# First block of a two-block layer: query and key head norms moved into the first stick-breaking steps, gate halves respaced over both attention loops, stick-breaking branch projected ahead of the latent one

## What is computed

```python
u = rms_norm(h, mix_norm[i])
proj = u @ w_in[i]
c_q, c_kv, k_rope, sb_qkv, gates = jnp.split(proj, SPLITS, axis=-1)
q = (rms_norm(c_q, q_latent_norm[i]) @ w_q_up[i])        # 8 heads of 96
kv = (rms_norm(c_kv, kv_latent_norm[i]) @ w_kv_up[i])    # 8 heads of 64 + 64
q = rms_norm(q, q_head_norm[i]); k = rms_norm(k, k_head_norm[i])
# rotary on the last 32 of each head, then causal softmax attention -> o_mla
sq, sk, sv = ...                                          # 8 heads of 64
o_sb = stick_breaking_attention(sq, sk, sv)
g_mla, g_sb = jnp.split(jax.nn.sigmoid(gates), 2, axis=-1)
merged = g_mla * (o_mla @ w_branch_mla[i]) + g_sb * (o_sb @ w_branch_sb[i])
h = h + merged @ w_out[i]
```

## Time and profile before

| | |
|---|---|
| median of 3 runs | 1412.13 us (1408.71 to 1412.49) |
| profiled execution | 1411.69 us, of which 1409.8 us are the span |
| TensorE busy | 1337.0 us (95%) |
| VectorE busy | 942.5 us (67%) |
| ScalarE busy | 767.1 us (54%) |
| GpSimd busy | 202.6 us (14%) |

### The profile page before, as it was taken

The page is one execution under the profiler, slowest core; times in us unless marked ns, Lnnn a source line. Parts: engine busy times, 40 slices in busy tenths (PEclk is TensorE's granted clock), DMA queues, the critical chain, the costliest instruction groups (busy, mean ns, idle before and its releaser), DMA issues.

```text
span 1409.8 us, 23082 instructions
## 1 busy us (share of the span) xinstructions
PE 1337.0 (95%) x9022; PEld 1217.7 (86%) x9022; DVE 942.5 (67%) x1369; ACT 767.1 (54%) x1150; POOL 202.6 (14%) x165
## 2 busy tenths in 40 slices
PE   9999999999899999999978997989999999999998
PEld 8999989879888999988977887879999877777876
DVE  6555574485476555566379674674675799999996
ACT  5433355664455333456354766324744577777774
POOL 1111120030001221110021321420001000202020
PEclk9999999999999999999989999989999899999999
DMA  9655535522346555544523332315364499999991
GB/s 314 209 179 182 191 122 177 185 90 68 120 150 192 181 182 189 169 135 147 189 89 122 119 124 98 101 38 176 124 210 154 163 409 369 335 367 339 374 332 58
DMA packets 73943, 263.44 MB, mean 187 GB/s; under 512 B 8320, under 2 KB 9600, under 8 KB 73728
## 3 DMA queue, kind: packets, MB, share of 16 engines
q1 hardware_dynamic: 72864, 260.39, 54.3%
q10 hardware_dynamic: 992, 1.86, 0.4%
HBM read 261.17 MB, written 1.05 MB: 186 GB/s over the span
## 4 chain that ended last, share of the span: by engine, by line
PE 59%; DVE 13%; ACT 6%; issue 2%; POOL 1%; DVEq 0%; ACTq 0%; POOLq 0%
PE bank L561 18%; PE bank L563 17%; PE bank L562 17%; DVE sb_wlo L518 3%; DVE sb_wlo L505 3%; DVE sb_XC L2103 1%; PE bank L2754 1%; ACT sb_Uh L636 1%; ACT sb_aw L1713 1%; ACT sb_whi L489 1%; PE bank L2811 1%; PE bank L653 1%; PE bank L741 0%; ACT sb_XC L1684 0%; PE bank L2729 0%
## 5 line engine op out<-in xcount | busy, mean ns | idle before, releaser
L505 DVE TENSOR_TENSOR sb_wlo<-sb_raw,sb_whi 128x1024 fp32r<-128x1024 f32 (+2 forms) x304 | 384.0, 1307 | 206.9 <-ACT sb_whi L489 206.7
L489 ACT ACTIVATE sb_whi<-sb_raw 128x1024 fp32r<-128x1024 f32 (+3 forms) x308 | 301.8, 1031 | 242.4 <-PE bank L563 236.0
L561 PE MATMUL bank<-sb_Uh,sb_whi 128*128 128x256 f32 x1216 | 349.0, 287 | 6.0 <-ACT sb_sgh L1677 2.5
L562 PE MATMUL bank<-sb_Ul,sb_whi 128*128 128x256 f32 x1216 | 344.9, 284 | 0.0
L563 PE MATMUL bank<-sb_Uh,sb_wlo 128*128 128x256 f32 x1216 | 344.9, 284 | 0.0
L561 PEld LDWEIGHTS bank<-sb_Uh,sb_whi 128*128 128x128 f32 x1216 | 234.3, 193 | 10.4 <-issue 6.3
L562 PEld LDWEIGHTS bank<-sb_Ul,sb_whi 128*128 128x128 f32 x1216 | 234.3, 193 | 0.9
L563 PEld LDWEIGHTS bank<-sb_Uh,sb_wlo 128*128 128x128 f32 x1216 | 234.1, 193 | 0.0
L561 PE MATMUL bank<-sb_whi,sb_Uh 128*128 128x256 f32 (+3 forms) x560 | 163.9, 293 | 6.7 <-DVE sb_Ul L645 4.9
L562 PE MATMUL bank<-sb_wlo,sb_Uh 128*128 128x256 f32 (+3 forms) x560 | 161.7, 289 | 0.0
L563 PE MATMUL bank<-sb_whi,sb_Ul 128*128 128x256 f32 (+3 forms) x560 | 161.5, 288 | 0.0
(11 more groups left out here) (405 smaller groups left out, 2261.0 us busy)
## 6 DMA issues: line engine op xcount, KB each, us to landing
sb_raw<-in_slabs SPq DMA_DIRECT2D x162, 512.0 KB, 4.7
sb_raw<-in_ffn_in SPq DMA_DIRECT2D x88, 512.0 KB, 4.5
sb_raw<-in_moe_in SPq DMA_DIRECT2D x50, 512.0 KB, 5.8
sb_raw<-in_ffn_out SPq DMA_DIRECT2D x44, 512.0 KB, 3.9
sb_raw<-in_moe_out SPq DMA_DIRECT2D x26, 512.0 KB, 6.1
sb_deep_free<-in_moe_in SPq DMA_DIRECT2D x16, 512.0 KB, 5.5
sb_deep_uh<-in_moe_in SPq DMA_DIRECT2D x16, 512.0 KB, 5.4
sb_deep_ul<-in_moe_in SPq DMA_DIRECT2D x16, 512.0 KB, 6.1
```

The source lines that it names most:

```text
L489: nc.scalar.activation(whi[:, i % NSLOT, c], raw[:, i % NSLOT, c], ACT.Copy).then_inc(S("hi_done"), 1)
L505: nc.vector.tensor_tensor(wlo[:, i % NSLOT, c], raw[:, i % NSLOT, c], whi[:, i % NSLOT, c].bitcast(F32), ALU.subtract).then_inc(S("lo_done ...
L561: pe.matmul(o, lh, rh, start=start, stop=False, skip_group_check=True)
L562: pe.matmul(o, lh, rl, start=False, stop=False, skip_group_check=True)
```

## The change

It edits orders and tables. (1) ScalarE squares the query heads before the loop: token tile 0 ahead of the split behind the query copies, token tile 1 between the key and value copies of tile 0 and of tile 1. VectorE sums them and GpSimd takes their root ahead of the loop. (2) The key squares and sums move to steps 0 and 1, query scaling, gain and rotation to steps 2, 3 and 4, the key's to 5, 6 and 7. (3) Gate halves: seven instead of six in the stick-breaking loop, at steps 0, 1, 2, 4, 6, 8 and 10, and nine instead of ten in the latent attention, at -1, 0, 1, 3, 4, 6, 7, 8 and 9; copies and splits follow (`gate_seen`, `late_seen`). (4) Gate 3 and the turned heads use other banks. (5) The stick-breaking branch is projected ahead of the latent one in each pair, with slabs to match.

```diff
@@ -124,7 +124,7 @@
     for i in range(2):
-        for nm, w in (("mla", "w_branch_mla"), ("sbr", "w_branch_sb")):
+        for nm, w in (("sbr", "w_branch_sb"), ("mla", "w_branch_mla")):
             add(f"{nm}{i}", w, i * 512, (i + 1) * 512, 4)
@@ -1354,10 +1354,12 @@
-        gate_bank = (6, 7, 6, 7, 2, 7, 2, 7)
-        gate_half_at = {0: (0, 0), 1: (0, 1), 2: (1, 0), 3: (1, 1), 5: (2, 0), 7: (2, 1)}
-        gate_seen = {2: 0, 4: 1, 8: 2}
-        qt_bank, kt_bank = (0, 1, 6, 7), (2, 3, 0, 1)
+        gate_bank = (6, 7, 6, 6, 2, 7, 2, 7)
+        gate_half_at = {0: (0, 0), 1: (0, 1), 2: (1, 0), 4: (1, 1), 6: (2, 0), 8: (2, 1), 10: (3, 0)}
+        gate_seen = {2: 0, 5: 1, 9: 2}
+        late_half_at = {-1: (3, 1), 0: (4, 0), 1: (4, 1), 3: (5, 0), 4: (5, 1), 6: (6, 0), 7: (6, 1), 8: (7, 0), 9: (7, 1)}
+        late_seen = {0: 3, 1: 4, 4: 5, 7: 6, 9: 7}
+        qt_bank, kt_bank = (0, 1, 2, 7), (3, 2, 7, 4)
@@ -1529,6 +1531,8 @@
                                    ACT.Copy).then_inc(S("q_ev"), 1)
+            act.wait_ge(*reach("q_ev", 4))
+            act_head_squares("hq", Q1, MH, QK, None, (0,))
             hi_upto("kvup")
@@ -1536,7 +1540,8 @@
                     act.activation(V1[:, t, 4 * half:4 * half + 4, :], b[:, :, NOPE:P], ACT.Copy).then_inc(S("kv_ev"), 1)
-            act.wait_ge(*reach("q_ev", 4))
+                if t == 0:
+                    act_head_squares("hq", Q1, MH, QK, None, (1,))
             act.wait_ge(*reach("kv_ev", 8))
@@ -1560,10 +1565,8 @@
                 if i < 2:
-                    act_head_squares("hq", Q1, MH, QK, None, (i,))
-                elif i < 4:
                     act.wait_ge(*reach("krope", 1))
-                    act_head_squares("hk", K1[:], MH, QK, ("hq_red", 2), (i - 2,))
+                    act_head_squares("hk", K1[:], MH, QK, ("hq_red", 2), (i,))
                 if i in gate_seen:
@@ -1578,10 +1581,10 @@
             def gates_seen(i):
-                if i % 2 == 0 and 0 <= i < 10:
-                    g = 3 + i // 2
+                if i in late_seen:
+                    g = late_seen[i]
                     gate_out(g)
-                    hi_upto(f"gate{g + 1}" if g < 7 else "mla0")
+                    hi_upto(f"gate{g + 1}" if g < 7 else "sbr0")
@@ -1592,7 +1595,7 @@
             for q in range(4):
-                hi_upto(f"sbr{q // 2}")
+                hi_upto(f"mla{q // 2}")
                 act.wait_ge(*reach("mg_s", q + 1))
@@ -1927,6 +1930,7 @@
             dve.wait_ge(*reach("ld_pb", 16))
+            dve_head_sums("hq", MH, QK)
             lo_upto("gate0")
@@ -1943,20 +1947,20 @@
                                              ALU.add).then_inc(S("sb_m"), 1)
-                if i < 4:
-                    dve_head_sums(("hq", "hk")[i // 2], MH, QK, (i % 2,))
+                if i < 2:
+                    dve_head_sums("hk", MH, QK, (i,))
+                elif i == 2:
+                    dve_head_rsqrt("hq", Q1, MH, QK)
+                elif i == 3:
+                    dve_head_gain("hq", Q1, MH, QK, "q_head_norm")
                 elif i == 4:
-                    dve_head_rsqrt("hq", Q1, MH, QK)
-                elif i == 5:
-                    dve_head_gain("hq", Q1, MH, QK, "q_head_norm")
-                elif i == 6:
                     dve.wait_ge(*reach("rope1", 2))
                     dve_rope("hq", Q1, MH, NOPE, ROPE // 2, COS1, SIN1)
+                elif i == 5:
+                    dve_head_rsqrt("hk", K1[:], MH, QK)
+                elif i == 6:
+                    dve_head_gain("hk", K1[:], MH, QK, "k_head_norm")
                 elif i == 7:
-                    dve_head_rsqrt("hk", K1[:], MH, QK)
-                elif i == 8:
-                    dve_head_gain("hk", K1[:], MH, QK, "k_head_norm")
-                elif i == 9:
                     dve.wait_ge(*reach("hq_turn", 6))
@@ -1972,14 +1976,14 @@
             def gates_low(i):
-                if i % 2 == 1 and 0 < i < 11:
-                    g = 3 + i // 2
-                    lo_upto(f"gate{g + 1}" if g < 7 else "mla0")
+                if i - 1 in late_seen:
+                    g = late_seen[i - 1]
+                    lo_upto(f"gate{g + 1}" if g < 7 else "sbr0")
...
             for q in range(4):
-                lo_upto(f"sbr{q // 2}")
-                used(dve, f"sbr{q // 2}")
+                lo_upto(f"mla{q // 2}")
+                used(dve, f"mla{q // 2}")
                 dve.wait_ge(*reach("gsig", 4))
@@ -2376,11 +2380,12 @@
                 pool_rsqrt(v, v, n, "lat_r")
+            pool_head_rsqrt("hq", MH, QK)
             for i in range(8):
...
                 pool.tensor_tensor(aw[:, 2 + i % 2], aw[:, 2 + i % 2], const("earlier"), ALU.mult).then_inc(S("sb_spm"), 1)
-                if i in (1, 3):
-                    pool_head_rsqrt(("hq", "hk")[i // 2], MH, QK)
+                if i == 1:
+                    pool_head_rsqrt("hk", MH, QK)
             pool_norm("n3")
@@ -2549,12 +2554,12 @@
             def gates_beside(i):
-                if i < 9:
-                    gate_half(3 + (i + 1) // 2, (i + 1) % 2)
+                if i in late_half_at:
+                    gate_half(*late_half_at[i])
...
             for j in range(2):
-                for nm, oh, ol, b0, done in (("mla", OMh, OMl, 0, "mg_a"), ("sbr", OSh, OSl, 4, "mg_b")):
+                for nm, oh, ol, b0, done in (("sbr", OSh, OSl, 4, "mg_b"), ("mla", OMh, OMl, 0, "mg_a")):
                     pe.wait_ge(*reach("mla_olo" if nm == "mla" else "os_lo", 4))
```

## The result

| | before | after |
|---|---|---|
| median | 1411.34 us (4 runs, 1408.71 to 1412.49) | 1401.41 us (4 runs, 1399.77 to 1402.78) |
| profiled execution | 1411.69 us | 1399.77 us |
| ratio of the times | | 0.9929, 95% interval 0.9917 to 0.9942 |

A forecast was written before the change was run, and what follows sets the result against it. TensorE, busy 95%, was taken as the bound, so only waits and slow clock could go: 4.29 + 6.20 - 0.75 = 9.74 us off the profiled 1411.69, plus 0.44 to the median, gives 1402.4 us, range 1399 to 1406.5.

The forecast's parts named there:

- End of the latent attention: Latent tail and first branch projection: waits of 3.74 us and slow clock of 2.46 go, 6.20 us off.
- End of the stick-breaking loop: Head turns and last value pairs: waits of 2.84 us and slow clock of 1.45 go, 4.29 us off.
- The second step: End of the stick-breaking loop: a gate half of 2.97 us is longer than the 1.86 us wait it must cover.
- the banks: Turned query and key heads in other banks: covered by the gate half of step 10, costed at nothing.
- Start of the loop: First gate half: an added query square delays ScalarE's copy freeing bank 6; 0.75 us lost, bounds 0.75 to 1.6.
- The sum: Whole kernel: 4.29 + 6.20 - 0.75 = 9.74 us off, giving 1402.4 us; chance 0.66.
- Middle of the loop: Mid stick-breaking loop: VectorE in time despite earlier work, tightest at step 6's score pair, margin 1.1 or 0.3 us; no cost.
- Rival C: Stick-breaking steps 3 to 7: VectorE late where splits run beside GpSimd; 3 us back, 1405.4 us; chance 0.12.
- End of the branch projections: VectorE's merge sets the 1.78 us wait and both ends move alike; nothing gained, nothing lost.
- B: Head turns: the clock still falls if the transposes alone cause it; 1.45 us stays, 1403.8 us; chance 0.10.
- D: Latent projection: OMl or its slab late, TensorE waits, clock falls again; 6.20 us stay, 1408.6 us; chance 0.09.
- E: Latent steps: ScalarE's and VectorE's steps outlast TensorE's, each head pays; slower, 1418.4 us at 2 us a head; chance 0.03.

The follow-up runs named there:

- e1: The kernel before with only the branch order turned round, stick-breaking ahead of latent; median 1405.63 us, ratio 0.9968 against before.
- e6: The changed kernel with the nine latent gate halves packed into steps -1 to 7; median 1404.11 us, ratio 0.9950 against the kernel before.
- e4: The changed kernel with the old branch order, latent projection first; median 1407.54 us, ratio 0.9971 against the kernel before.
- e2: The kernel before with only the query and key norms moved earlier; gates, banks and branch order as before; median 1413.84 us, ratio 1.0020 against before.
- e11: The changed kernel with the query and key norms put back where they were before; median 1400.18 us, ratio 0.9925 against the kernel before.
- e7: The changed kernel with the gate half of stick-breaking step 10 moved to latent step -1; median 1405.04 us, ratio 0.9956 against the kernel before.
- e3: The changed kernel with the square of query tile 1 behind all key and value copies; median 1400.88 us, ratio 0.9928 against the kernel before.
- e8: The changed kernel with gate 0 in bank 4 instead of bank 6; median 1398.37 us, ratio 0.9910 against the kernel before.
- e9: As e8, with the transposes of p in bank 4 instead of bank 6; median 1398.12 us, ratio 0.9913 against the kernel before.
- e10: As e9, with VectorE's merge written for two parts at a time; median 1398.69 us, ratio 0.9912 against the kernel before.
- e5: The changed kernel with gate halves and banks as before, so norms and branch order alone; median 1409.14 us, ratio 0.9978 against the kernel before.

## Why the prediction was right, and where it was off

**End of the latent attention, 6.20 us.** Right. The latent and branch parts are 9.04 us shorter, of which one gate half, 2.97, only moved: 6.07 us. e1 shows the 2.47 of wait and the slow clock to hang on the branch order. e6 shows that without the halves at steps 8 and 9 the tail waits again, 2.37 us at the last turn. e4 shows that the new halves need the new order at this place: with the old one the wait is 4.85 us, more than the 3.74 of before. The margin for OMl was put at 0.5 us and is 0.89.

**End of the stick-breaking loop, 4.29 us.** The amount is right, the explanation only in part. The waits fell from 2.84 to 0.20 us and the slow clock of 1.45 us is gone, 4.09 us. The prediction laid the waits to VectorE reaching the key heads late, "since sums, scaling, gain and rotation of query and key stand in its steps 0 to 9". That VectorE was late is right; moving this work forward was not the remedy. Done alone (e2) it leaves waits of 1.29 and 2.13 us; left out beside the new gate tables (e11), no wait stands there at all. The second step, that a half of 2.97 us covers the wait of 1.86, fails too: e7 has no such half and no wait for OSl. The half at step 10 covers other things, the exponential of head 7 and the key turn. What the traces show in place of both is the split of the next gate slab, 2.36 us, right ahead of OSl in VectorE's step 8 before and in e2, and behind it wherever the new tables are in. The new banks add to it: with the old ones the first latent scores wait for the third copy of the turned keys, with the new ones for the first, some 1.1 us apart (2.02 against 0.93 us in e2 and after). The prediction put the banks at nothing. No run moves the split alone or the banks alone, so these two shares are read from the traces and not tested.

**A term not seen.** The value pairs of heads 6 and 7, apart before and ready together behind the half of step 10, take 0.81 us together where two apart take 1.60: 0.79 us more off.

**Start of the loop, 0.75 us.** The step was right and its size wrong, by a term left out. The wait grew by 0.72 us as worked out, but the clock fell behind it, which costs another 1.48: 2.20 in all, beyond the upper bound of 1.6. The bounds were made of waits alone, although the prediction priced slow clock at both other places. e3 and e11 bring the wait back to 1.10 us and e8 removes it, by three different edits, and the clock stays at 1.00 in all three. Why it falls behind this wait is not shown. Here the Trainium skill (TensorE: Matmul & The Clock Gate, Terms) is nearer than it was at the places of the earlier trace rows: half of 3.30 us is 1.65, against 1.48 measured, in a stretch that TensorE filled.

**The sum.** 4.09 + 0.79 + 6.07 - 2.20 = 8.75 us; the stretch shows 8.86. The forecast of 9.74 was 0.9 too high there. The median moved by 9.93, and the 1.1 us between are not explained by the changed part; the runs after vary by 3.0 us, and the clock outside the stretch varies with them. So the close hit of 1402.4 is partly two errors of opposite sign, and partly luck.

**Middle of the loop, nothing.** Right: no wait in mid-loop, and 0.20 us at the first latent scores. The margin at the score pair of step 6 was put at 1.1 us, or 0.3 if a split runs slow beside GpSimd; it is 0.30, but for another reason: the split there took 2.35 us, as priced, while the query scaling took 2.31 where 1.75 was taken. That this meets the 0.3 is luck. Rival C was that close.

**End of the branch projections, nothing.** Right: 1.68 us against 1.78, and e9 and e10 show VectorE's merge chain to be what sets it.

**The rivals.** B fell: 16 query and 16 key transposes run at clock 1.00 once no long wait stands between them. C, D and E did not happen; e4 is what D describes, a wait for OMl with a fall of the clock.

**What stays open.** Why the clock fell behind the wait of 1.82 us in five of the six kernels that have it, and not in e2. How the gain at the end of the stick-breaking loop divides among the split's place, the halves and the banks. And whether the norms' cost of 2.65 us of stretch shows in the time: e11's median is 1.2 us below the changed kernel's, inside both intervals; e2 against before does show it.

## What to carry to other kernels

When several edits serve one purpose, time each alone and each left out. Here the gate tables and the branch order carry all of the gain, and each is worth more beside the other: the order 6.26 us of stretch with the new tables and 4.88 without, the tables 7.02 with the new order and 123.48 - 119.35 = 4.13 without. The norms, the largest edit, cost time in each of the three pairs that were run (e2 against before, e5 against e1, after against e11). When an engine is late with what another waits for, read its timeline just ahead of that instruction: here a split stood there that served something else, and moving the work that seemed to be late only moved the wait. And price any wait that an edit lengthens with the slow clock that can follow it, at its start as well as where it removes one.

## What was not expected of the hardware

- **Two value pairs together.** The matmuls of heads 6 and 7 write 64 partitions each, to the two halves of one bank. Issued one behind the other with their data ready, both pairs took 0.81 us after, and 314.66 - 313.85 = 0.81 in e11, against 0.80 for a single pair. At the end of the latent attention, where the pairs stand next to each other too, they hardly did: 360.51 - 359.86 = 0.65, then 361.30 - 360.51 = 0.79. What differs there was not tried. The Trainium skill (TensorE: Matmul & The Clock Gate, Part 3: Packing small matmuls — row/col tiling) says that small matmuls placed in different tiles of the array run at the same time; the first place agrees, the second does not show it.
- **Which waits the clock followed.** In this part of the kernel the clock fell to 0.50 at or right behind waits of 1.86 and 2.47 us (before), 1.82 (after, e4 to e7), 2.13 (e2, e5), 2.37 (e6) and 4.85 (e4). It stayed at 1.00 behind 1.78, 1.68 (after), 1.55 (e9), 1.41 (e10), 1.29 (e2), 1.28 (e7) and 1.10 us, and behind the 1.82 us of e2. The length of the wait sorts all but one of them.
